# A hybrid attention block on one core: tail loads in pieces of 512 columns, more loaded ahead, query tiles in one store, first activations first

## The chip, the cores and the metric

One core of one Trainium2 chip runs the whole kernel. The metric is the device time of one execution in microseconds (us), lower is better; three executions of the kernel before gave 3302.88, 3305.68 and 3307.67 us.

## The reference

One layer of a hybrid block on 2048 tokens of width 1024, in float32:

```
h    = rmsnorm(x, norm1_g) * (1 + sc1) + sh1          # sc1, sh1, g1, ...: six rows of silu(c) @ w_ada + b_ada
proj = h @ w_in                                       # 1024 -> 3280 columns: aq ak av bq bk bv iq ik iw
A: 4 heads, two softmax maps each, softmax(q1 k1) - lam * softmax(q2 k2), times av, ALiBi, causal in chunks of 64
B: score[t,s] = sum over 16 heads of iw[t,h] * relu(iq[t,h] . ik[s]);  keep the 256 best keys of each query
   8 heads attend to these keys (one shared bk, bv), ALiBi
x = x + g1 * (concat(A, B) @ w_out)
x = x + g2 * (relu(h2 @ w_ff1)^2 @ w_ff2);  out = rmsnorm(x, final_g)
```

The factors on the norm and lambda parameters change only the inputs' values.

## The kernel before, in words

Matrices are multiplied as three products of two-part operands (high times high, high times low, low times high), so most tiles exist as a pair "hi" and "lo". Four stages follow each other; the instruction streams of the five engines are written out in order, and a stage ends when all of them are through.

**Index projection** (`index_projection`). x comes in four groups of 512 tokens (`xt`, two buffers). For each group ACT sums the squares (`squares`), DVE and ACT make 1/rms (`variance`, `root`, `inverse`), x is scaled, PE transposes it (`turn`, 8 slices k of 128 columns, in two parts of four), and DVE and ACT apply scale and shift and split the result into `ht_hi` and `ht_lo` (DVE's `activations`, ACT's `first_parts`, slice by slice, even slices made by DVE, odd by ACT). The scale and shift come from w_ada: DVE forms weighted sums (`ada_sums`, four first chunks of 512 columns), PE sums over partitions (`columns`), and `norm_cols` (L475) finishes them. `split_w` splits a weight tile on ACT and DVE. Then `unit(n, i, g)` multiplies weight tile i by token group g, 24 matmuls of 512 columns. There are nine weight tiles (the 1024 columns of iq, then ik, bv's upper part and iw in the others) and so 36 units; the first three tiles run group by group while the next group is being made. Each result is evacuated as hi (ACT) and lo (DVE, L437) and stored to DRAM by SP as four transfers of 64 rows (L333). SP's queue is in order: a store waits for its lo part, and the load of group 3 of x (L329) stands behind the stores of units 0 to 2. The last transfer of SP is that of the gates (L336).

**Indexing** (`indexing`). PE computes the remaining 17 tiles of the projection (544 steps of three matmuls, L1098) and, between them, the index scores of blocks 2 to 15 (a block is 128 queries): scores on PE (L1082), relu on ACT (L1143), weighted sum on DVE into `rank` (L1237); for blocks 2 to 11 a search for the 256th value in 24 rounds follows (ACT L1150, DVE L1258). SP loads `iq` in units of two heads (two transfers of 128 KB); unit n waits until unit n-3 has been used. POOL issues everything else: weights, stores of the tiles (four transfers each, L1023; the four av tiles one each into `scr.av`), the finished score rows of blocks 12 to 15 (`keep`, L1035), and when the last tile is stored `load_values` (L966: av by groups of 512 tokens with three of its four row tiles in one transfer, the fourth tile's columns 512 to 2047 in one, bv in three) and `load_ahead` (L987: queries of the first two attention units and the first 512 columns of bk and of six of the eight ak tiles). PE turns av and bv (`vturn`, L1114 to L1130; bv with 32 matmuls of 64 columns), ACT copies them (L1159). The order of all this on PE, ACT, DVE and POOL is written out by a planner (`indexing_streams`, `indexing_plan`): it starts, among the next steps of all streams, the one that can begin first, begins rounded to `INDEX_SLACK`, ties by a key that `INDEX_PLACES`, `REST_FROM`, `REST_PACE`, `ROUNDS` and `INDEX_MASK` set. The waits in the code keep it right whatever the plan.

**Attention** (`attention`). A second planner orders 16 blocks of 6 groups: scores (L3024), maxima (L3255), exponentials (L3091), the difference of the two maps (`combine`, L3265 to L3271), transposes (L3040), products with values (L3055, L3061), stores of the result to `dram_mix` (L2994). Score units of four heads are loaded by SP (L2933, two transfers of 256 KB, three buffers); SP also loads the missing keys (L2942). Unit 0 and unit 1 are those of group A, unit 2 the first of group B. The searches of blocks 12 to 15 run between: POOL fetches the row of block 12 as `rank_in` at once (L2975), DVE starts on it at L3167.

**Output and MLP** (`output_mlp`) is not touched.

## Time and profile before

| | us |
|---|---|
| median of three executions | 3305.68 |
| profiled execution, its own time | 3311.04 |
| span of its trace | 3309.3 |
| index projection, PE's first matmul to the next stage's | 10.0 to 296.4 |
| indexing, to the first matmul of attention | 296.4 to 961.9 |
| attention, output projection and MLP | 961.9 to 3309.3 |

A row of a timeline gives the start, the duration, the engine, the line, the operation, output and input, the count of merged instructions, and in brackets how long the engine was idle before and what released it. "SPq" and "POOLq" are queues that issue transfers; "PEq" is PE's own instruction queue. The granted clock of TensorE is either full (a 512-column matmul then shows 0.39 us and starts every 0.23 us) or half (0.63 us, every 0.43 us).

### The profile page before, as it was taken

The page shows a single profiled execution, that of the slowest core. Times are in us where ns is not written, and L with a number is a line of the kernel's source. Part 1 is how long each engine was busy: PE and PEld are TensorE (multiplying, and loading weights), DVE is VectorE, ACT ScalarE, POOL GpSimd, SP SyncE. Part 2 cuts the span into 40 slices and gives each one's busy share as a digit, 9 for nine tenths or more (in the row PEclk, how much of TensorE's full clock was granted, in tenths as well). Part 3 has the DMA queues.
Part 4 walks back from the last instruction along what each step waited for, and adds up shares of the span by engine and source line. Part 5 has one row for each costly group of instructions (what it writes and reads, how often), then busy time and mean ns, then how long its engine had stood idle before and what let it go on. Part 6 is the DMA issues. An engine that isn't in the chain of part 4 may idle for free. (4 is left out here: it accounts for less than half of the span.)

```text
span 3309.3 us, 44362 instructions
## 1 busy us (share of the span) xinstructions
PE 3132.8 (95%) x15808; PEld 2544.1 (77%) x15808; DVE 2439.7 (74%) x4302; ACT 1847.5 (56%) x3103; POOL 442.0 (13%) x713
## 2 busy tenths in 40 slices
PE   5899999999978999999999999999999999999998
PEld 4787888888756777777777787788778878888787
DVE  5544898999956687878776678787877875655676
ACT  4312888899768989898986334322432232222232
POOL 0011233012221000000000000221121210000321
PEclk9999999999979999999999999999999999999999
DMA  7476544233376432211111463544444456655555
GB/s 241 128 247 164 150 135 116 84 102 100 120 204 148 102 74 51 60 43 52 33 38 73 140 221 128 188 150 159 145 163 151 161 196 227 240 188 187 194 203 198
DMA packets 327002, 471.73 MB, mean 143 GB/s; under 512 B 25344, under 2 KB 214992, under 8 KB 326400
## 3 DMA queue, kind: packets, MB, share of 16 engines
q1 hardware_dynamic: 274768, 296.96, 30.0%
q0 software_dynamic: 52016, 171.96, 15.5%
q8 instruction: 125, 2.05, 0.3%
q14 instruction: 93, 0.76, 0.1%
HBM read 311.84 MB, written 156.98 MB: 142 GB/s over the span
## 5 line engine op out<-in xcount | busy, mean ns | idle before, releaser
L2513 PE MATMUL m_ps<-m_h,w_hi 128*128 128x512 f32 x1792 | 557.8, 393 | 20.0 <-DVE w_lo L2115 11.9
L2513 PEld LDWEIGHTS m_ps<-m_h,w_hi 128*128 128x128 f32 x1792 | 338.0, 189 | 95.8 <-DVE w_lo L2115 16.4
L1237 DVE SCALAR_TENSOR_TENSOR rank<-spare,iw,rank 128x1024 f32<-128x1024 f32 (+5 forms) x330 | 331.4, 1021 | 37.9 <-ACT spare L1143 31.3
L2526 PE MATMUL m_ps<-w_hi,a_hi 128*128 128x512 f32 x896 | 350.1, 391 | 6.3 <-DVE w_lo L2344 3.4
L2513 PE MATMUL m_ps<-m_h,w_lo 128*128 128x512 f32 x896 | 350.9, 392 | 0.0
L2526 PE MATMUL m_ps<-w_lo,a_hi 128*128 128x512 f32 x896 | 349.8, 390 | 0.0
L2526 PE MATMUL m_ps<-w_hi,a_lo 128*128 128x512 f32 x896 | 349.6, 390 | 0.0
L1143 ACT ACTIVATE spare<-isps 128x1024 f32<-128x1024 f32 (+5 forms) x352 | 277.6, 820 | 60.7 <-PE isps L1082 37.4
L1082 PE MATMUL isps<-ki,iq 128*128 128x512 f32 (+3 forms) x1216 | 291.4, 373 | 11.9 <-DMA iq<-dram_proj 8.8
L1082 PEld LDWEIGHTS isps<-ki,iq 128*128 128x128 f32 x1216 | 224.6, 190 | 67.4 <-DMA iq<-dram_proj 11.4
L1819 ACT ACTIVATE a_hi<-a_lo 128x2048 fp32r<-128x2048 f32 x56 | 107.3, 1917 | 279.3 <-DMA a_lo<-dram_aop 279.3
L3103 ACT ACTIVATE pt<-tps 128x512 f32<-128x512 f32 (+1 forms) x432 | 232.3, 584 | 55.3 <-PE ops L3055 26.6
L3040 PE MATMUL tps<-ident,probs 128*128 128x128 f32 x1632 | 236.6, 280 | 22.7 <-DVE probs L3271 17.6
L1781 ACT ACTIVATE w_hi<-w_raw 128x512 fp32r<-128x512 f32 x160 | 99.8, 625 | 264.1 <-DVE w_raw L2103 205.2
L3091 ACT ACTIVATE probs<-probs,stat 128x128 f32<-128x128 f32 (+15 forms) x192 | 233.1, 1217 | 20.0 <-DVE stat L3255 17.2
L3040 PEld LDWEIGHTS tps<-ident,probs 128*128 128x128 f32 x1632 | 182.1, 142 | 78.4 <-issue 35.2
L1150 ACT ACTIVATE below<-rank,tk 128x512 int8<-128x512 f32 (+9 forms) x210 | 230.4, 1100 | 19.2 <-DVE tk L1259 18.1
L2341 DVE TENSOR_TENSOR a_lo<-a_lo,a_hi 128x2048 fp32r<-128x2048 f32 x56 | 141.3, 2524 | 113.9 <-ACT a_hi L1819 113.8
L1098 PE MATMUL r_ps<-ht_hi,r_w_hi 128*128 128x512 f32 x544 | 216.4, 398 | 6.0 <-PEq L270 4.9
L1694 POOL DMA_DIRECT2D dram_aop<-a_out x224 | 121.0, 541 | 748.5 <-ACT a_out L1803 275.5
L1098 PE MATMUL r_ps<-ht_hi,r_w_lo 128*128 128x512 f32 x544 | 214.5, 394 | 0.0
L1098 PE MATMUL r_ps<-ht_lo,r_w_hi 128*128 128x512 f32 x544 | 213.8, 393 | 0.0
(317 smaller groups left out, 6594.4 us busy)
## 6 DMA issues: line engine op xcount, KB each, us to landing
w_raw<-in_w_ff SPq DMA_DIRECT2D x136, 512.0 KB, 5.5
dram_aop<-a_out POOLq DMA_DIRECT2D x224, 256.0 KB, 2.6
a_lo<-dram_aop SPq DMA_DIRECT2D x56, 1024.0 KB, 5.6
early_queries<-dram_proj SPq DMA_DIRECT2D x124, 256.0 KB, 4.3
iq<-dram_proj SPq DMA_DIRECT2D x224, 128.0 KB, 2.9
ada_w<-in_w_ada POOLq DMA_DIRECT2D x16, 1024.0 KB, 6.4
dram_proj<-r_ev_hi POOLq DMA_DIRECT2D x104, 128.0 KB, 2.6
dram_proj<-r_ev_lo POOLq DMA_DIRECT2D x104, 128.0 KB, 2.7
```

What stands on the lines that cost most here:

```text
L1082: mm = nc.tensor.matmul(sps[:, job.n % 2, a:b], iq[:, job.unit % IQU, job.head % 2, part, :], ki[:, job.c * SCH + a:job.c * SCH + b], star ...
L1098: mm = nc.tensor.matmul(ps[:, job.n % 4, :], a[:, i % 2, job.part, :], b[:, job.g, job.part, :], start=job.part == 0 and m == 0, stop=job. ...
L1143: nc.scalar.activation(spare[:, job.n % 2, 0:job.width], sps[:, job.n % 2, 0:job.width], ACT.Relu).then_inc(s_relu, 1)
L1150: nc.scalar.activation(below[:, q, 0:length].bitcast(I8), ranks[job.k % 3][:, 0:length], ACT.Sign, bias=tk[:, q, TK_NT:TK_NT + 1], accum_o ...
L1237: nc.vector.scalar_tensor_tensor(out=dst, in0=got, scalar=w, in1=dst, op0=ALU.mult, op1=ALU.add).then_inc(s_acc, 1)
L1694: pool.dma_start(scr.aop[op, row:row + P, half * GT:(half + 1) * GT], act_in[:, op, :]).then_inc(q_a[op], 16)
L2341: nc.vector.tensor_tensor(s_lo[:, c % RING], s_lo[:, c % RING].bitcast(F32), s_hi[:, c % RING].bitcast(F32), ALU.subtract).then_inc(c_sl, 1)
L2513: mm = nc.tensor.matmul(ps[:, b], w[:, w1_slot(n, j), k, :], hop[:, j, h, :, k, :], start=fresh and k == 0 and i == 0, stop=k == KH - 1 an ...
L2526: mm = nc.tensor.matmul(ps[:, t], a[:, c % RING, k, t * P:(t + 1) * P], w[:, c % RING, k, :], start=first and i == 0, stop=last and i == 2 ...
L3040: tr = nc.tensor.transpose(tps[:, job.turn % TR, (2 * kk + hh) * P:(2 * kk + hh + 1) * P], probs[:, g.heads[hh] % 4, (job.first + kk) * P: ...
L3091: nc.scalar.activation(row, row, ACT.Exp, bias=stat[:, job.hm % 8, 2:3], scale=-1.0, accum_out=stat[:, job.hm % 8, 3:4]).then_inc(s_exp, 1)
L3103: nc.scalar.activation(pt[:, job.slot % PT, 0:width], tps[:, job.of.turn % TR, 0:width], ACT.Copy).then_inc(s_te, 1)
```

## The change

Query tiles of the projection are kept in DRAM by part (`by_part`: 128 rows of hi, then 128 of lo) and stored by one transfer of 512 KB in place of four of 128 KB; the six tiles with keys, bv and iw keep four. The loads of queries read the new arrangement, with as many transfers and bytes as before. In the projection's start ACT takes the first activations before the squares of group 1, `inverse(0)` and `columns(3)` come earlier, and `split_w(0)` on DVE comes behind the first activation. The tail loads of indexing fetch the fourth av tile and bv in pieces of 512 columns; bv lies with hi on partitions 0 to 63 and lo on 64 to 127, and is turned by 16 matmuls with two identities stacked in place of 32. `load_ahead` takes three units, seven ak tiles and the score row of block 12. The planner's constants of indexing are new. `fac` is made by one scalar_tensor_tensor. Left out below: `stored_by`, the changed indices of `queries` and `iq` in loads and matmuls, and places in SBUF.

```diff
-INDEX_SLACK = 0.0347
-REST_FROM, REST_PACE, ROUNDS, INDEX_MASK = 75.86, 12.486, -34.794, 169.04
-INDEX_PLACES = dict(index=-17.19, relu=-566.8, add=26.95, chain0=-84.64, chain1=-82.32, keep=-267.36, split=258.6,
-                    lo=110.56, mm=-14.26, evac=-14.83, evac_lo=-191.95, store=-481.49, kept_mask=-573.36,
-                    weights=-212.32, vload=20.2, ahead=-14.8, vturn=-70.63, vcopy=31.74)
+INDEX_SLACK = 0.0636
+REST_FROM, REST_PACE, ROUNDS, INDEX_MASK = 132.07, 8.185, -26.461, 168.05
+INDEX_PLACES = dict(index=-10.95, relu=-518.06, add=-25.25, chain0=-91.79, chain1=-87.39, keep=-319.67, split=239.2,
+                    lo=191.27, mm=29.75, evac=-79.21, evac_lo=-185.88, store=-387.22, kept_mask=-566.03,
+                    weights=-221.42, vload=-82.91, ahead=56.8, vturn=-270.56, vcopy=-9.75)
...
+        self.by_part = self.proj.rearrange("(c m) r p t -> c (m r p) t", m=2)
...
+KEY_TILES = [*range(R_AK // P, R_AK // P + 4), R_BK // P, CT - 1]
+
+
+def stores_of(tile):
+
+    return 4 if tile in KEY_TILES else 1
+
+
+def store_tile(eng, scr, tile, tok, hi, lo, both, s):
+
+    if tile not in KEY_TILES:
+        eng.dma_start(scr.by_part[tile, :, tok].rearrange("(r p) t -> p r t", p=P), both.bitcast(F32)).then_inc(s, 16)
+        return
+    for part, src in enumerate((hi, lo)):
+        for half in range(2):
+            eng.dma_start(scr.proj[tile * P // DH + half, part, :, tok],
+                          src[half * DH:(half + 1) * DH, :].bitcast(F32)).then_inc(s, 16)
+
...
+        self.rank = sb("rank", [P, SEQ])
...
-        ev_hi = sb("ev_hi", [P, EV, GT], F32R)
-        ev_lo = sb("ev_lo", [P, EV, GT], F32R)
+        ev = sb("ev", [P, EV, 2, GT], F32R)
+        ev_hi, ev_lo = ev[:, :, 0, :], ev[:, :, 1, :]
...
-                    for part, src in enumerate((ev_hi, ev_lo)):
-                        for half in range(2):
-                            sp.dma_start(scr.proj[INDEX_TILES[i] * P // DH + half, part, :, g * GT:(g + 1) * GT],
-                                         src[half * DH:(half + 1) * DH, n % EV, :].bitcast(F32)).then_inc(s_st[n % EV], 16)
+                    store_tile(sp, scr, INDEX_TILES[i], slice(g * GT, (g + 1) * GT), ev_hi[:, n % EV, :],
+                               ev_lo[:, n % EV, :], ev[:, n % EV], s_st[n % EV])
...
-                squares(1, range(0, 2))
                 act.wait_ge(s_cols, 1)
-                first_parts(0, range(KT))
-                squares(1, range(2, TG))
+                first_parts(0, range(KT - 2))
+                squares(1, range(0, 1))
+                first_parts(0, range(KT - 2, KT))
+                squares(1, range(1, TG))
                 root(1)
...
-                def ada_sums(at, h):
+                def ada_sums(at, h, between=None):
...
+                        if between and k == (h + 1) * KH - 2:
+                            between()
...
+                        if g == 0 and k == 1:
+                            split_w(0)
...
-                ada_sums(2, 1)
-                inverse(0)
+                ada_sums(2, 1, lambda: inverse(0))
                 for h in range(2):
                     ada_sums(3, h)
-                split_w(0)
...
-                def turn(g, part):
+                def turn(g, part, halves=(0, 1)):
                     pe.wait_ge(s_xn, TG * (g + 1))
-                    for k in range(part * KT // 2, (part + 1) * KT // 2):
+                    first = part * KT // 2
+                    for k in range(first + halves[0] * KT // 4, first + (halves[-1] + 1) * KT // 4):
...
-                turn(0, 0)
+                turn(0, 0, (0,))
                 columns(3)
+                turn(0, 0, (1,))
                 turn(0, 1)
...
-EARLY_KEYS, EARLY_UNITS = 6, 2
+EARLY_KEYS, EARLY_UNITS = 7, 3
...
-    for n, (count, late) in enumerate(((2, 6.0), (2, 11.0), (1, 14.0), (1, 17.0), (3, 21.0))):
+    for n, (count, late) in enumerate(((2, 6.0), (2, 9.0), (2, 13.0), (2, 17.0), (4, 21.0))):
...
-    put("ahead", Step("ahead", "Q", 13.0, 9.0, REST_FROM + REST_PACE * (len(REST_TILES) + 6), [(loads[-1], -21.0)]))
+    put("ahead", Step("ahead", "Q", 16.0, 8.0, REST_FROM + REST_PACE * (len(REST_TILES) + 6), [(loads[-1], -20.0)]))
...
-        turn = put("vturn", Step("vturn", "PE", 0.55 if n < NB else 1.26, 0.163, where, after, n=n))
+        turn = put("vturn", Step("vturn", "PE", 0.55 if n < NB else 0.63, 0.163, where, after, n=n))
...
-        low_b = early.queries[0:DH, QU - 1].rearrange("p m r q -> p (m r q)")
+        def sparse_rows(g):
+
+            return early.ka[:, NG, g * GT:(g + 1) * GT] if g else early.ka[:, EARLY_KEYS - 1, GT:2 * GT]
+
...
-                    elif n == 1:
-                        pool.dma_start(early.kb[:, GT:].bitcast(F32), scr.av[3 * P:, GT:]).then_inc(s_vin[1], 16)
-                    elif n == NG:
-                        row = scr.proj[R_BV // DH]
-                        pool.dma_start(low_b.rearrange("p (r t) -> p r t", r=2).bitcast(F32),
-                                       row[:, :, 0:GT].rearrange("r p t -> p r t")).then_inc(s_vin[NG], 16)
-                        for part in range(2):
-                            pool.dma_start(early.ka[0:DH, NG + part, GT:].bitcast(F32),
-                                           row[part, :, GT:]).then_inc(s_vin[NG], 16)
+                    elif n < NG:
+                        tok = slice(n * GT, (n + 1) * GT)
+                        pool.dma_start(early.kb[:, tok].bitcast(F32), scr.av[3 * P:, tok]).then_inc(s_vin[n], 16)
+                    else:
+                        for g in range(NG):
+                            tok = slice(g * GT, (g + 1) * GT)
+                            pool.dma_start(sparse_rows(g).bitcast(F32),
+                                           scr.proj[R_BV // DH, :, :, tok].rearrange("r p t -> (r p) t")
+                                           ).then_inc(s_vin[NG], 16)
...
-                        row = early_units[n] // DH
-                        view = scr.proj[row:row + 4, :, :, 0:P].rearrange("m r p q -> p (m r) q")
+                        row = early_units[n] // P
+                        view = scr.by_part[row:row + 2, :, 0:P].rearrange("c (x p) q -> p (c x) q", p=DH)
                         for half in range(2):
-                            pool.dma_start(early.queries[half * DH:(half + 1) * DH, n].rearrange("p m r q -> p (m r) q")
+                            pool.dma_start(early.queries[half * DH:(half + 1) * DH, n].rearrange("p c r m q -> p (c r m) q")
                                            .bitcast(F32), view).then_inc(s_ahead, 16)
...
+                    pool.wait_ge(s_kept[(SPLIT - 2) % 3], 16)
+                    for a in range(0, P * (SPLIT + 1), GT):
+                        b = min(a + GT, P * (SPLIT + 1))
+                        pool.dma_start(early.rank[:, a:b], scr.ranks[0, :, a:b]).then_inc(s_ahead, 16)
...
-                                pe.wait_ge(s_idr, 1)
-                                pe.wait_ge(s_vin[NG], 48)
+                                pe.wait_ge(s_idr, 2)
+                                pe.wait_ge(s_vin[NG], 16 * NG)
                             for m in range(8):
                                 kt = 8 * (n - NB) + m
-                                for part in range(2):
-                                    if kt < 4:
-                                        rows = low_b[:, part * GT + kt * P:part * GT + (kt + 1) * P]
-                                    else:
-                                        rows = early.ka[0:DH, NG + part, kt * P:(kt + 1) * P]
-                                    mm = nc.tensor.matmul(ps[:, n % 4, m * DH:(m + 1) * DH], rows, ident_r[:],
-                                                          start=part == 0, stop=part == 1, skip_group_check=True)
+                                rows = sparse_rows(kt // 4)[:, kt % 4 * P:(kt % 4 + 1) * P]
+                                mm = nc.tensor.matmul(ps[:, n % 4, m * DH:(m + 1) * DH], rows, ident_r[:],
+                                                      start=True, stop=True, skip_group_check=True)
...
-                nc.scalar.activation(ident_r[:], keep.ident[0:DH, 0:DH], ACT.Copy).then_inc(s_idr, 1)
+                for half in range(2):
+                    rows = slice(half * DH, (half + 1) * DH)
+                    nc.scalar.activation(ident_r[rows, :], keep.ident[rows, rows], ACT.Copy).then_inc(s_idr, 1)
...
-                if job.kind == "fetch":
-                    if job.block > SPLIT:
-                        pool.wait_ge(s_mask, job.block - SPLIT)
+                if job.kind == "fetch" and job.block > SPLIT:
+                    pool.wait_ge(s_mask, job.block - SPLIT)
...
-                    dve.wait_ge(s_rank, 16 * (job.block - SPLIT + 1))
+                    if job.block > SPLIT:
+                        dve.wait_ge(s_rank, 16 * (job.block - SPLIT))
...
-                    then(nc.vector.tensor_scalar(fac[:], stat[:, a, 3:4], rinv[:, r, 1:2], keep.neg_lam[:],
-                                                 ALU.mult, ALU.mult))
+                    then(nc.vector.scalar_tensor_tensor(out=fac[:], in0=stat[:, a, 3:4], scalar=rinv[:, r, 1:2],
+                                                        in1=keep.neg_lam[:], op0=ALU.mult, op1=ALU.mult))
```

## Rows read from the trace of the kernel before

**Rows 1.** The page, engines: busy time, share of the span, instructions.
```profile
PE 3132.8 (95%) x15808; PEld 2544.1 (77%) x15808; DVE 2439.7 (74%) x4302; ACT 1847.5 (56%) x3103; POOL 442.0 (13%) x713
```

**Rows 2.** Windows: stretch, length, busy time by engine, clock, DMA share, GB/s.
```profile
150.00:200.00 50.00, 50.00 (x228) 40.70 (x227) 22.90 (x32) 7.53 (x11) 6.41 (x8) 1.00 0.75 243
...
296.40:961.00 664.60, 650.48 (x2972) 534.21 (x2972) 583.91 (x1161) 555.58 (x875) 159.25 (x278) 0.99 0.45 127
...
950.00:960.00 10.00, 9.85 (x71) 8.59 (x70) 7.15 (x6) 8.44 (x13) 0.56 (x1) 1.00 0.13 52
```

**Rows 3.** Timeline, start of the projection.
```profile
39.80 3.68 PE L605 MATMUL tps<-ident,xt_first 128*128 128x128 f32 x16 [2.52 <-ACT xt_first L397]
...
41.32 1.22 DVE L431 TENSOR_TENSOR w_lo<-w_raw,w_hi 128x1024 fp32r<-128x1024 f32 x1
...
43.27 1.71 PE L614 MATMUL col_psum<-ones,ada_sums 128*128 128x1 f32 x8
...
45.75 0.81 DVE L532 TENSOR_SCALAR u<-tps,cols 128x512 f32<-128x512 f32 x1 [0.29 <-DVE cols L473]
...
48.87 1.06 ACT L367 ACTIVATE ada_first<-xt 128x1024 f32<-128x1024 f32 x1 [6.95 <-DMA xt<-in_x]
...
51.10 0.61 ACT L386 ACTIVATE ht_hi<-u 128x512 fp32r<-128x512 f32 x1
...
55.71 0.78 PE L593 MATMUL ps<-ht_hi,w_hi 128*128 128x512 f32 x1
...
59.23 0.39 PE L593 MATMUL ps<-ht_hi,w_lo 128*128 128x512 f32 x1
...
61.17 0.69 DVE L536 TENSOR_TENSOR ht_lo<-u,ht_hi 128x512 fp32r<-128x512 f32 x1 [0.80 <-ACT ht_hi L386]
```

**Rows 4.** Timeline, the load of the last group of x and PE's wait.
```profile
92.32 0.59 SPq L329 DMA_DIRECT2D xt<-in_x  x1
...
101.21 1.06 ACT L367 ACTIVATE ada_first<-xt 128x1024 f32<-128x1024 f32 x1 [5.87 <-DMA xt<-in_x]
...
115.69 3.67 PE L605 MATMUL tps<-ident,xt 128*128 128x128 f32 x16 [3.96 <-DVE xt L516]
```

**Rows 5.** Timeline, from the projection to indexing.
```profile
294.02 1.23 SPq L333 DMA_DIRECT2D dram_proj<-ev_lo  x2
...
296.40 0.76 PE L1098 MATMUL r_ps<-ht_hi,r_w_hi 128*128 128x512 f32 x1 [4.90 <-PEq L270]
```

**Rows 6.** Timeline, PE in the tail of indexing.
```profile
931.87 2.85 PE L1082 MATMUL isps<-ki,iq 128*128 128x512 f32 x8 [3.24 <-DMA iq<-dram_proj]
...
943.00 1.90 PE L1082 MATMUL isps<-ki,iq 128*128 128x512 f32 x4 [4.72 <-DMA iq<-dram_proj]
...
957.52 2.84 PE L1130 MATMUL r_ps<-ident_v,early_ka 64*128 64x64 f32 x24
```

**Rows 7.** DMA queues, 925 to 930, then 930 to 935: packets, MB, share.
```profile
q0 software_dynamic: 392, 1.48, 91.6%
q1 hardware_dynamic: 392, 0.19, 14.5%
...
q0 software_dynamic: 205, 0.92, 91.2%
q1 hardware_dynamic: 204, 0.10, 14.0%
```

**Rows 8.** Timeline, start of attention.
```profile
963.18 0.54 POOL L2975 DMA_DIRECT2D rank_in<-dram_ranks  x1 [0.36 <-issue]
...
973.98 0.69 PE L3024 MATMUL sps<-early_kb,early_queries 128*128 128x128 f32 x2 [6.17 <-DMA early_queries<-dram_proj]
...
984.19 0.63 ACT L3115 ACTIVATE mixst<-ops,rinv 128x128 f32<-128x128 f32 x2 [3.15 <-DMA dram_mix<-mixst]
...
984.96 1.08 PE L3055 MATMUL ops<-pt,early_vb 128*64 128x256 f32 x2 [2.39 <-ACT mixst L3115]
```

**Rows 9.** Groups of instructions: busy us, mean ns, idle before.
```profile
L3268 DVE TENSOR_SCALAR fac<-stat,rinv,neg_lam 128x1 f32<-128x1 f32 x64 | 17.5, 273 | 2.3
```

50 lines of the change are left out of this document (25 added, 25 removed).

## The prediction

> **What bounds the kernel now.** I read the page first: PE is busy for 95% of the span [rows 1], so time is won where PE waits, where it runs at the lower of its two clocks, or where it is given less to do. Then I read the windows for such places: 50.00 us of 50 in the projection's even part, 650.48 of 664.60 us through indexing, at a mean granted clock of 0.99 [rows 2]. DVE has 583.91 and ACT 555.58 us in the same stretch, so neither is far below. Indexing is thus bound by PE except in its tail. Then timelines of the seams. Four of them have PE idle and are touched by the change: the projection's start [rows 3], its last group of x [rows 4], the step to indexing [rows 5], and the tail of indexing with the start of attention [rows 6 to 8]. MLP, a third of the span, is untouched, and nothing there depends on when it starts.
>
> **Start of the projection.** The first real matmul starts at 55.71 [rows 3]. Behind it stands ACT: the first slice of activations `u` is there at 45.75 + 0.81 = 46.56, but ACT splits it at 51.10 only, because in its order the squares of group 1 come first and these wait 6.95 us for x, which lands at 48.87. The change takes this wait away. What is late next: `u` itself. It waits for `columns(3)`, which PE does behind 16 transposes (39.80 to 43.27), while the sums it needs are ready at 41.32. With 8 transposes ahead of it and `inverse(0)` earlier, `columns(3)` begins at about 41.4 in place of 43.27; DVE then does not put `split_w(0)` (1.22) ahead, but that was hidden beside `columns(3)` anyway. So `u` starts at 45.75 - 1.85 = 43.9, and ACT splits at 44.7, 6.4 us earlier than 51.10. `split_w(0)` now stands behind the first `u`: 44.7 to 45.95, and holds the first low part back by 0.5 us (the high part is done at 44.7 + 0.61). The slices thus come 5.9 us earlier, the first matmul at about 49.8. Of slices 6 and 7 one group of squares is now ahead, 1.05 to 1.25 us: the last low part moves from 61.17 to 61.17 - 5.9 + 1.1 = 56.4. The clock: PE was at the lower level until 59.23, 3.5 us after the first matmul; the same 3.5 us at half speed from 49.8 give 53.3, 5.9 earlier, and the remaining matmuls (16 at 0.23, 3.7 us) then end at 57.0, just where the last low part (57.1) allows it, so unit 0 ends some 5.2 us earlier. x of group 1 is scaled at about 63 in place of 66.8, while PE wants it at 63.3: hidden, and 0.4 us late at worst. Term: -5.2; bounds: -3.5 (slices 6 and 7 and the scaling both late) and -6.4.
>
> **Last group of x.** SP issues this load at 92.32, behind the four transfers of unit 2's store; it lands after 8.9 us, ACT waits 5.87 us for it, and at the end of that chain PE waits 3.96 us at 115.69 [rows 4]. Three of four issues of that store go. One costs 1.23 / 2 = 0.6 us [rows 5], so the load starts 1.8 to 2.2 us earlier, and PE's wait falls to about 1.8. PE then did 16 transposes in 3.67 us at the lower clock, as in [rows 3], where full clock would make it about half. Whether 1.8 us of idling is short enough to keep the full clock no row tells; if it is, another 1.8 to 2.1 us go. Term: -2.2, the nearest row being the wait itself; bounds -1.5 and -4.3. The Trainium skill, "TensorE: Matmul & The Clock Gate", Part 1, says that idling is what sends the clock back and that this depends on when the gap comes; by it the shorter gap would more often keep full clock, and the sum would be -4. The 3.96 us gap with 3.67 us behind it agrees with the first half.
>
> **Step to indexing.** PE waits 4.90 us until 296.40, when SP has issued its last transfers [rows 5]. Three issues of 0.6 us fall away: -1.8, bounds -1.2 and -2.3. The store's own landing is later awaited with the gates' in one wait and moves with it. Between the first and the last unit the fewer issues are worth nothing: PE is full (50.00 of 50) [rows 2] and covers them.
>
> **The body of indexing.** The same 32 stores of query tiles become one transfer each; POOL is busy for 159.25 us of 664.60 and nobody on the path waits for it. The planner's new constants reorder the streams. By the keys the scores still go ahead of the projection's matmuls, and the search ahead of the sums, so most of the order stays. PE's work is the same and only its 14.1 us of idling [rows 2] could go, of which 8 belong to the tail. I take 0; bounds -5 (most of the rest goes) and +6 (1% of the stage, less than DVE's reserve of 66 us under PE makes impossible).
>
> **Tail of indexing.** PE waits 3.24 and 4.72 us for `iq` while POOL's mass of loads runs [rows 6]. The packets show how: from 925 to 930 the two queues moved 392 packets each, from 930 to 935 205 and 204 [rows 7]. They take turns packet by packet, so `iq`, cut in packets of 0.5 KB, gets as many turns as POOL's queue has packets, and these were 3.8 and 4.5 KB long. A unit of `iq` has 512 packets, 6.5 us at the first rate and 12.5 us at the second. In pieces of 512 columns the fourth av tile comes in packets of 2 KB in place of 6, bv in 512 packets in place of 192: about 580 more turns before the heavy queries, more than one unit. That says both waits shrink, the second least, since a third unit of queries (128 packets of 4 KB) now stands ahead too. I take 3 of the 8 us (bounds: 8 gone, 3 more). The last bv matmuls, 24 in 2.84 us [rows 6], halve with the others: 32 x 0.118 / 2 = 1.9 us less, with the copies of ACT waiting for them. Against this stands a new hold: the extra loads are 512 + 256 + 832 KB = 1.6 MB, at 334 or 204 GB/s [rows 7] 4.8 to 7.8 us. The transfers were through by 950 (share 0.13 after it) [rows 2]; now they last to 955 to 958, and POOL waits for them at the stage's end. PE's end would be 960.4 - 4.9 = 955.5. So of 4.9 us I count 4. Bounds: +2 (`iq` later by 3, bv's 1.9 kept, loads late) and -7. The Trainium skill, "DMA: Bandwidth & Descriptors", Bandwidth, speaks against cutting loads up: it wants 1 MiB a transfer and gives some 2 us fixed for each, by which three transfers of 256 KB for one of 768 KB would add about 4 us, and the tail's gain would be nothing. Here the engines are full to 91% on POOL's queue alone [rows 7], so fixed times lie beside other transfers.
>
> **Start of attention.** PE waits 6.17 us for the queries of the third unit, behind 832 KB of `rank_in` and keys [rows 8]. Both are now there beforehand: the wait goes. What is late next are the queries of the fourth unit: PE wants them about 7 us after the third, at 974 to 975 on the old clock, and SP issues them some 2 us into the stage; even 9 us to landing would do. ACT then waited 3.15 us for a store to land in the crowded queues, and PE 2.39 us for ACT [rows 8]; with 1.6 MB fewer in these 20 us half of that should go. Term: -6.2 - 1.3 = -7.5; bounds: -3 and -9.
>
> **The rest.** `fac`: 64 instructions of 273 ns, 17.5 us in all [rows 9], beside PE for the most part; 0, bounds -2 and +2. Two ACT copies for the stacked identities, 0.3 us at a time when ACT waits for weights: 0. The search's first instruction waits no longer, and did not wait before.
>
> **The sum.** -5.2 - 2.2 - 1.8 + 0 - 4 - 7.5 + 0 = -20.7 us. The profiled execution had 3311.04 us of its own; it becomes 3290.3. The median of the runs shown is 5.4 us below the profiled one, which gives 3285.
>
> **Rivals.** (1) The loads ahead hold the stage's end: the engines are through, POOL still waits for the last piece of the score row. For it: 1.6 MB more into queues at 91% [rows 7]. Against: 10 us with hardly a transfer before the end [rows 2]. The tail then gives +2 in place of -4: 3291. (2) Attention's start gives nothing: the wait moves to the fourth unit. For it: its queries share the queues with three keys. Against: 832 KB less ahead of it. 3285 + 7.5 = 3292. (3) All goes better: full clock kept at group 3 (-2), both `iq` waits gone and PE's idling in indexing too (-7): 3276. (4) Slower: the new order of indexing makes PE wait for DVE or ACT. Its place is 296 to 961, where PE now has a ready matmul nearly always [rows 2]; a loss of 3.1% of that stage, 20.7 us, is the point from which it decides, and with DVE at 88% and ACT at 84% of it, twice this is possible: 41 us, giving 3305.7 - 20.7 + 41 = 3326. For it: several constants changed by tens of blocks. Against: keys decide only among steps that begin within 0.06 us. (5) The first term fails, because PE's later waits in the projection (3.96 us) hang on DMA landing at a fixed time and not on PE: 3290.
>
> **How the numbers follow.** The forecast 0.52, its own range 3279 to 3291; rival 1 0.14, rival 2 0.11, rival 3 0.11, rival 4 0.06, rival 5 0.06. A measurement tells 0.2%, 6.6 us, from no change: faster is below 3299.1. The forecast, 1, 2, 3 and 5 are faster, but half of 1 and 2 could meet a loss of 5 us in the body of indexing, and some of those end within 0.2%: faster 0.86, same 0.08, slower 0.06. The range 3275 to 3297 leaves out rival 4, the upper end of 1 and 2 and the lower end of 3.
>
> **What would show it.** `ht_hi` first split near 44.7 and the first long matmul near 50; a wait of about 2 us or less before the transposes of the last group; 3 us between PE's last projection matmul and indexing, not 4.9; waits for `iq` in the tail under 5 us in all, 16 bv matmuls; no wait for queries of the third unit, and transfers ending within 3 us of the stage's end. It is wrong if the body of indexing has more PE idling than 6 us outside the tail, if a wait of over 4 us for other queries opens in attention, or if the four seams together give less than 12 us.

## The result and the profile after

The changed kernel takes 3286.02 us (median of 4 runs, 3284.53 to 3286.66), the kernel before beside it 3306.68 (4 runs, 3302.88 to 3308.01): the ratio is 0.9935, 95% interval [0.9924, 0.9947], 20.7 us less. Forecast were 3285 and the same 20.7 us. (Timed a second time, `e1_after` below, the difference of the medians was 22.6.) The execution that was profiled took 3285.41 us, span 3283.6, 25.7 less than the span before. Those 5 us more than the medians give are mostly the old trace's: traced a second time (`e3_before_again`, below), the kernel before had a span of 3305.6, and 22.0 us are left.

The page's engine line and windows of the changed kernel, against [rows 1, 2]. The second window runs from indexing's first matmul to attention's:

```profile
PE 3126.7 (95%) x15792; PEld 2535.0 (77%) x15792; DVE 2433.2 (74%) x4302; ACT 1847.0 (56%) x3104; POOL 401.4 (12%) x626
```

```profile
150.00:200.00 50.00, 50.00 (x229) 40.72 (x228) 26.86 (x36) 8.52 (x12) 7.19 (x9) 1.00 0.70 234
283.41:945.61 662.20, 647.57 (x2956) 529.05 (x2956) 582.49 (x1163) 556.24 (x879) 120.32 (x192) 0.99 0.43 130
940.00:945.00 5.00, 0.76 (x7) 0.64 (x6) 0.00 (x0) 1.29 (x3) 0.00 (x0) 0.68 1.00 393
```

PE has the same work less 16 matmuls and is as full as before in both long stretches. POOL is busy 38.9 us less in indexing, where the stores now take fewer issues; PE is no fuller for it. The third row is new: 5 us before attention in which PE does almost nothing and the transfers run at 393 GB/s. Not all of these are loads ahead. The DMA view of the same 5 us has 461 packets, 1.97 MB, and only 349 of them lie under 8 KB:

```profile
DMA packets 461, 1.97 MB, mean 393 GB/s; under 512 B 93, under 2 KB 93, under 8 KB 349
```

The other 112 have the 8 KB of a row of the last score row's store (block 15, 128 rows of 2048 columns, `keep`), which POOL issued at 937.51. They are 0.92 MB, nearly half of the bytes; the stage's end doesn't wait for this store, but it shares the engines with the loads that it does wait for.

The timeline of the changed kernel from the projection's start to its end, against [rows 3 to 5]:

```profile
40.72 1.87 PE L641 MATMUL col_psum<-ones,ada_sums 128*128 128x1 f32 x8 [1.13 <-DVE ada_sums L492]
...
43.10 0.81 DVE L560 TENSOR_SCALAR u<-tps,cols 128x512 f32<-128x512 f32 x1
...
44.01 0.63 ACT L409 ACTIVATE ht_hi<-u 128x512 fp32r<-128x512 f32 x1 [2.75 <-DVE u L560]
...
48.55 0.48 PE L619 MATMUL ps<-ht_hi,w_hi 128*128 128x512 f32 x1
48.87 0.39 PE L619 MATMUL ps<-ht_lo,w_hi 128*128 128x512 f32 x1
...
54.92 0.69 DVE L564 TENSOR_TENSOR ht_lo<-u,ht_hi 128x512 fp32r<-128x512 f32 x1 [0.64 <-ACT ht_hi L409]
...
92.67 1.06 ACT L390 ACTIVATE ada_first<-xt 128x1024 f32<-128x1024 f32 x1 [3.83 <-DMA xt<-in_x]
...
107.14 1.97 PE L632 MATMUL tps<-ident,xt 128*128 128x128 f32 x16 [1.39 <-DVE xt L542]
...
282.03 0.36 SPq L113 DMA_DIRECT2D dram_proj<-ev  x1
...
283.41 0.77 PE L1130 MATMUL r_ps<-ht_hi,r_w_hi 128*128 128x512 f32 x1 [2.77 <-PEq L295]
```

`ht_hi` is split 7.1 us earlier than in [rows 3], the first long matmul comes 7.2 us earlier. PE's wait for the last group of x is 1.39 us in place of 3.96 [rows 4], and the 16 transposes behind it take 1.97 us in place of 3.67. The step to indexing costs 2.77 us in place of 4.90 [rows 5], with one transfer of `ev` on SP where there were four. Indexing starts 13.0 us earlier.

The timeline at the tail and at attention's start, against [rows 6, 8], and then the group of `fac`, against [rows 9]:

```profile
921.95 3.78 PE L1114 MATMUL isps<-ki,iq 128*128 128x512 f32 x8 [2.76 <-DMA iq<-dram_proj]
...
938.78 1.97 PE L1158 MATMUL r_ps<-ident_v,early_ka 128*128 128x64 f32 x16
...
945.04 0.29 DVE L3174 TENSOR_TENSOR early_table<-early_table,early_diagonal 128x128 f32<-128x128 f32 x1 [7.83 <-PEq L965]
...
945.61 2.97 PE L3054 MATMUL sps<-early_ka,early_queries 128*128 128x128 f32 x10 [4.86 <-ACT stack L3113]
```

```profile
L3299 DVE SCALAR_TENSOR_TENSOR fac<-stat,rinv,neg_lam 128x1 f32<-128x1 f32 x64 | 14.1, 220 | 2.3
```

The last turn of bv ends at 938.78 + 1.97 = 940.75, where it was 960.36. Then PE stands for 4.86 us, and DVE for 7.83: no engine starts attention before the loads ahead have landed. No wait for a third unit's queries is left. `fac` takes 220 ns in place of 273.

### The profile page after: what moved, and what is told of

Its sections match the earlier page's. It is cut to its first block and busy times, and to the rows that moved or that the text cites. A ratio compares the mean times of both kernels' runs of the same rounds, so it can differ in the third digit from the quotient of the medians.

```text
span 3283.6 us, 44143 instructions
## 1 busy us (share of the span) xinstructions
PE 3126.7 (95%) x15792; PEld 2535.0 (77%) x15792; DVE 2433.2 (74%) x4302; ACT 1847.0 (56%) x3104; POOL 401.4 (12%) x626
## 3 DMA queue, kind: packets, MB, share of 16 engines
q8 instruction: 125, 2.05, 0.3%
```

## The experiments

Each kernel was timed in 5 rounds. Beside the first four the kernel before had 3308.68 us (9 runs), beside the next four 3307.78 (11), beside the last four 3307.95 (15). A table first, in which every trace is cut in three: when indexing starts; PE's time in it (first matmul to the last turn of bv); the rest to the end of the span. For the kernel before that end is 957.52 + 2.84 [rows 6].

| kernel | indexing starts | PE in indexing | rest | median | ratio, interval |
|---|---|---|---|---|---|
| before | 296.40 | 664.0 | 2348.9 | 3306.68 | |
| e3_before_again | 296.07 | 665.3 | 2344.3 | 3308.14 | 1.0004 [0.9995, 1.0013] |
| changed | 283.41 | 657.3 | 2342.8 | 3286.02 | 0.9935 [0.9924, 0.9947] |
| e1_after | 283.02 | 659.1 | 2343.2 | 3286.13 | 0.9930 [0.9916, 0.9944] |
| e1_undo_start | 289.64 | 658.3 | 2341.8 | 3294.53 | 0.9957 [0.9943, 0.9971] |
| e1_four_stores | 289.72 | 656.9 | 2344.5 | 3290.57 | 0.9944 [0.9930, 0.9957] |
| e1_rank_wait_late | 284.16 | 656.6 | 2340.1 | 3283.28 | 0.9928 [0.9915, 0.9942] |
| e2_old_plan | 283.33 | 666.1 | 2336.8 | 3290.24 | 0.9949 [0.9934, 0.9964] |
| e2_no_ahead | 284.33 | 655.7 | 2344.1 | 3287.94 | 0.9942 [0.9925, 0.9959] |
| e2_rank_fetched_late | 286.20 | 658.3 | 2343.5 | 3287.88 | 0.9937 [0.9922, 0.9952] |
| e2_one_piece | 287.13 | 660.1 | 2340.9 | 3287.08 | 0.9936 [0.9920, 0.9952] |
| e3_later_waits | 284.01 | 659.4 | 2343.1 | 3289.84 | 0.9946 [0.9932, 0.9959] |
| e3_old_fac | 285.16 | 656.8 | 2340.1 | 3285.68 | 0.9937 [0.9923, 0.9950] |
| e3_before_new_plan | 294.88 | 671.0 | 2354.2 | 3321.89 | 1.0038 [1.0024, 1.0052] |

The intervals reach about 3 to 6 us to each side, so a part worth 2 us doesn't show in a ratio. Where a median is said to rise or fall below, it is against the 3286.13 of `e1_after`.

**The changed kernel again.**

> The changed kernel itself, timed beside the others and the kernel before. If the 25.7 us between the two traces are the whole effect, the medians differ by 25; if the kernel before was only unlucky in its profiled execution, by 20 to 21.

It came out at 3286.13 us, 22.6 below the kernel before beside it: nearer to the second reading than to the first. The seams up to indexing lie within 0.7 us of the changed kernel's, bv ends 1.4 us later, and attention's first scores waited 6.30 us in place of 4.86. So the hold of one and the same code varies by 1.4 us.

**The projection's start undone.**

```diff
-                act.wait_ge(s_cols, 1)
-                first_parts(0, range(KT - 2))
-                squares(1, range(0, 1))
-                first_parts(0, range(KT - 2, KT))
-                squares(1, range(1, TG))
+                squares(1, range(0, 2))
+                act.wait_ge(s_cols, 1)
+                first_parts(0, range(KT))
+                squares(1, range(2, TG))
```

with `inverse(0)`, `split_w(0)` and `columns(3)` back at their old places.

> Changed kernel, with only the order at the projection's start as it was (squares of group 1 first, split_w(0), inverse(0) and columns(3) in their old places). My account, by the sum of waits: first long matmul back near 55.5 and 6.5 us slower than the changed kernel. Rival, that later parts of the projection hang on transfers landing at fixed times: the first matmul moves, but the time by 3 us or less.

```profile
55.22 0.78 PE L618 MATMUL ps<-ht_hi,w_hi 128*128 128x512 f32 x1
...
88.11 3.38 PE L631 MATMUL tps<-ident,xt_first 128*128 128x128 f32 x16 [3.96 <-DVE xt_first L541]
...
289.64 0.76 PE L1128 MATMUL r_ps<-ht_hi,r_w_hi 128*128 128x512 f32 x1 [2.77 <-PEq L295]
```

The first long matmul is back at 55.22, group 2 is turned 6.4 us later than in `e1_after` (81.74), and indexing starts 6.6 us later. The median rose by 8.4, and the rival is out. The order of the start is worth 6.4 to 6.6 us at its own place and the kernel keeps it to the end.

**Four stores for a query tile in the projection.** The destination stays, cut in four:

```diff
-                    store_tile(sp, scr, INDEX_TILES[i], slice(g * GT, (g + 1) * GT), ev_hi[:, n % EV, :],
-                               ev_lo[:, n % EV, :], ev[:, n % EV], s_st[n % EV])
+                    store_in_four(sp, scr, INDEX_TILES[i], slice(g * GT, (g + 1) * GT), ev_hi[:, n % EV, :],
+                                  ev_lo[:, n % EV, :], s_st[n % EV])
```

> Changed kernel, with each tile of the index projection stored by SP in four transfers again, to the same places. My account: the load of the last group of x starts 1.8 to 2.2 us later, PE waits over 3 us before its transposes and is then at the lower clock (another 1.7 to 2.3 us), and the step to indexing is 2 us longer: 6 us slower in all. Rival, that the kept clock was chance and not the shorter wait: 4 us slower, and the 16 transposes still take 1.9 to 2.0 us.

```profile
109.39 3.68 PE L643 MATMUL tps<-ident,xt 128*128 128x128 f32 x16 [3.96 <-DVE xt L553]
...
289.72 0.76 PE L1141 MATMUL r_ps<-ht_hi,r_w_hi 128*128 128x512 f32 x1 [4.89 <-PEq L306]
```

Both waits of before are back to the hundredth, 3.96 and 4.89, and with the first of them the half clock on the transposes. Indexing starts 6.7 us later than in `e1_after`: 2.6 at the last group, 2.1 at the step, and the 1.9 between them is the clock. The median rose by 4.4. One trace can't tell the rival from my account, that the kept clock was chance: the table of nine traces below does that.

**The wait for the score row moved to its use.**

```diff
-                        pool.dma_start(early.rank[:, a:b], scr.ranks[0, :, a:b]).then_inc(s_ahead, 16)
+                        pool.dma_start(early.rank[:, a:b], scr.ranks[0, :, a:b]).then_inc(early.s_rank, 16)
```

> Changed kernel, but the score row loaded ahead has a semaphore of its own on which DVE waits where its search begins, and the stage's end no longer waits for it. My account (rival 1 of the prediction in part: PE now idles 4.86 us at the stage's end because the loads ahead have not landed): 832 KB at some 390 GB/s, the last in the queue, so the stage ends 2.1 us sooner and the kernel is 2 us faster. Rival, that the end is set by something else (the store of the last row, the keys): no change.

```profile
943.67 2.97 PE L3054 MATMUL sps<-early_ka,early_queries 128*128 128x128 f32 x10 [2.94 <-ACT stack L3113]
```

PE's wait fell from 4.86 and 6.30 to 2.94, and the median by 2.9 us: the size that was expected, but the interval doesn't tell it from nothing.

**The planner's old constants in the changed kernel.**

```diff
-INDEX_SLACK = 0.0636
+INDEX_SLACK = 0.0347
```

and the other constants of the change, likewise.

> Changed kernel with the planner's old constants for indexing (the costs of the streams stay new). My account: the body of indexing is bound by PE either way, 0 within 2 us. Rival: the new constants are what brings the tail forward (waits for iq 4.3 us in place of 8.8): 3 to 6 us slower, with iq waits of 7 us or more.

The waits of PE from the projection's end on, engine, line, waited for, then us in total, times, longest; the first fence is `e2_old_plan`, the second the changed kernel:

```profile
PE isps L1114 <- DMA iq<-dram_proj: 7.1, 6, 4.4
...
PE sps L3054 <- ACT stack L3113: 2.4, 1, 2.4
```

```profile
PE sps L3054 <- ACT stack L3113: 4.9, 1, 4.9
PE isps L1114 <- DMA iq<-dram_proj: 4.3, 2, 2.8
```

The rival held: waits for `iq` of 7.1 us, the median 4.1 us above `e1_after`'s, PE's time in indexing back at 666.1 us, the value of before. But the rest is the shortest of all, 2336.8. A part of that is the clock. These are windows of the 60 us behind the last turn of bv, `e2_old_plan`, then `e3_before_again`; the granted clock is the third number from the end:

```profile
949.46:1009.46 60.00, 47.13 (x237) 35.81 (x238) 36.11 (x171) 46.60 (x150) 7.58 (x15) 0.77 0.78 186
```

```profile
961.33:1021.33 60.00, 44.35 (x197) 33.92 (x197) 30.85 (x152) 40.47 (x131) 6.58 (x13) 0.64 0.79 180
```

With full clock as 1 and half as 0.5, a mean of 0.77 is 28 of the 60 us at half clock, 0.64 is 43. The changed kernel has 0.66 there (41 us), `e2_no_ahead` 0.72 (34).

**No more loaded ahead than before** (two units, six keys, the row of scores fetched in attention).

```diff
-EARLY_KEYS, EARLY_UNITS = 7, 3
+EARLY_KEYS, EARLY_UNITS = 6, 2
```

> Changed kernel with two units, six ak tiles and no score row loaded ahead, as before; the pieces of 512 columns stay. My account: PE's 4.86 us of idling at the stage's end falls to about 1.6, attention's start loses the 6.2 us for the third unit and the 2.4 to 3 us behind the store: 5 to 6 us slower in all. Rival, that the gain of attention's start came from elsewhere (fac, the order of stores): the third unit's wait is back, yet under 3 us slower.

```profile
941.60 0.66 PE L3051 MATMUL sps<-early_ka,early_queries 128*128 128x128 f32 x4 [1.55 <-ACT stack L3110]
...
954.19 0.69 PE L3051 MATMUL sps<-early_kb,early_queries 128*128 128x128 f32 x2 [6.79 <-DMA early_queries<-dram_proj]
```

The hold is gone (1.55 us) and the wait for the third unit's queries is back (6.79, against 6.17 in [rows 8]). The median rose by 1.8 us, inside the interval, where 5 to 6 were expected: the rival's number, though not for its reason. Loading ahead took 6.79 us of waiting away and put 3.3 us of hold in its place, 4.7 in the repetition. The clock was higher here (0.72 against 0.66, as said), so this trace's rest is the shorter for it.

**The score row alone fetched in attention.**

```diff
-                        pool.dma_start(early.rank[:, a:b], scr.ranks[0, :, a:b]).then_inc(s_ahead, 16)
```

> Changed kernel with only the score row of block 12 fetched at attention's start, as before. My account: the stage ends 2.1 us sooner, and the 832 KB then stand beside the queries of the fourth and fifth unit, where nothing waits for 6 us: within 1.5 us of the changed kernel. Rival, that it was the row and not the place in the order that held up the third unit's queries before: 3 us or more slower, with a new wait of PE for queries or of ACT for a store.

```profile
959.34 1.89 DVE L3194 TENSOR_REDUCE tk<-early_rank 128x1 f32<-128x1664 f32 x1 [3.06 <-DMA early_rank<-dram_ranks]
```

PE's wait at attention's start was 4.06 us, against 4.86 and 6.30. The search then waited 3.06 us for the row, and PE stood 5.56 us for DVE behind it, where the changed kernel has 2.53. The time is the same within 2 us.

**The fourth av tile in one piece again.**

```diff
-                        pool.dma_start(early.kb[:, tok].bitcast(F32), scr.av[3 * P:, tok]).then_inc(s_vin[n], 16)
+                        pool.dma_start(early.kb[:, GT:].bitcast(F32), scr.av[3 * P:, GT:]).then_inc(s_vin[1], 16)
```

> Changed kernel with columns 512 to 2047 of the fourth av tile loaded in one transfer again (rows of 6 KB). My account, that the two queues take turns packet by packet: 256 packets of POOL's queue fewer, so iq gets 256 turns fewer and PE waits for it 2 to 3 us more; of that 0 to 2 us reach the time, since the stage's end waits for the loads anyway. Rival, that pieces are worth nothing: iq waits as in the changed kernel, 4.3 us.

Two waits for `iq` of 2.79 and 2.43 us, 7.3 us in all over the stage against 4.3 in the changed kernel and 3.0 to 4.4 in the eight other traces that have both the new plan and the pieces. PE's time in indexing was 1 to 3 us longer than in the changed kernel and its repetition, the median 1 us. The waits grew as expected, but the count behind them was wrong. The pages count POOL's packets over the whole program, the changed kernel, then this one:

```profile
q0 software_dynamic: 51024, 172.74, 15.1%
```

```profile
q0 software_dynamic: 50928, 172.74, 15.1%
```

That is 96 packets fewer for the same bytes, and not 256: rows of 2 KB don't travel one to a packet (1.57 MB in 440 packets, 3.6 KB each, in the changed kernel from 915 to 920). At 440 packets in 5 us, 96 turns are an estimated 1.1 us of the 3 to 4; where the rest comes from isn't shown. The Trainium skill, "DMA: Bandwidth & Descriptors", Bandwidth, has the rule to make transfers large. No cost of the pieces shows here: in one piece the median is 1 us higher, inside the interval.

**Each load awaited where it is used.** Three semaphores in place of one; the stage's end waits for unit 0 and four keys only. The order of the loads changes with it: unit 0 and four keys, unit 1 and three keys, unit 2 and bk, the row, where the changed kernel loads all three units first.

```diff
-                pool.wait_ge(s_ahead, 16 * (1 + EARLY_KEYS + 2 * EARLY_UNITS + (P * (SPLIT + 1) + GT - 1) // GT))
+                pool.wait_ge(s_ahead, 16 * (2 + 4))
...
+                        if unit in (1, 2):
+                            pe.wait_ge(early.s_later[unit - 1], 16 * (2 + EARLY_KEYS - 4 if unit == 1 else 3))
```

> The changed kernel, with the end of indexing held only by what attention's first unit needs (its queries and four key tiles); the rest of the loads ahead (unit 1's queries and three keys, unit 2's queries and bk, the score row) is awaited where it is first used, each on a semaphore of its own. If the hold at the stage's end is what swallowed the gain of the tail, PE's wait ahead of attention's first scores falls from 4.9 us (6.3 in its repetition) to the 1.6 that it had with few loads ahead, the third unit finds its queries there, and the time is 3 to 4.5 us below the changed kernel, about 3282. Rival: the bytes are what is short, not the place of the wait; PE then meets the same wait at its second or third unit and 0 to 1 us is left.

```profile
944.92 2.81 PE L3064 MATMUL sps<-early_ka,early_queries 128*128 128x128 f32 x10 [1.55 <-ACT stack L3123]
...
953.33 0.69 PE L3064 MATMUL sps<-early_ka,early_queries 128*128 128x128 f32 x2 [4.47 <-DMA early_ka<-dram_proj]
```

The hold went (1.55) and stood again 8 us later, 4.47 us, for a key, and at 966.20 PE waited 3.02 us more behind ACT. The median, 3289.84, is 3.7 above `e1_after`'s. The rival held: with this order of loads the bytes are short, not the place of the wait. In its windows, 940 to 965 in steps of 5 us, the DMA engines are full throughout, at shares of 1.02 to 1.17 (the column before the last); two of them:

```profile
940.00:945.00 5.00, 3.44 (x30) 3.12 (x29) 0.40 (x2) 4.52 (x11) 0.56 (x1) 1.00 1.03 206
...
950.00:955.00 5.00, 1.68 (x8) 1.68 (x9) 0.84 (x6) 0.72 (x4) 0.00 (x0) 0.50 1.03 365
```

**The new constants alone, in the kernel before.** The reverse of `e2_old_plan`'s edit, and nothing else.

> The kernel before with the planner's new constants alone. By the run with the old constants in the changed kernel, they are worth 4 us: PE's time from the first matmul of indexing to the last should fall from 664.0 us towards 657, and as no new loads hold the stage's end here, the time falls by 4 to 7 us against the kernel before, to about 3302. Rival, as I had it in the prediction: the constants give nothing by themselves, only with the smaller pieces and the single stores; then 0 to 1 us.

Neither: 3321.89 us, 13.9 slower than the kernel before, its interval clear of 1. From its timeline, PE, POOL, PE:

```profile
931.96 0.40 PE L1098 MATMUL r_ps<-ht_hi,r_w_lo 128*128 128x512 f32 x1
...
940.04 0.79 POOL L972 DMA_DIRECT2D early_ka<-dram_av  x1 [2.68 <-DMA dram_proj<-r_ev_lo]
...
973.21 2.10 PE L3024 MATMUL sps<-early_ka,early_queries 128*128 128x128 f32 x7 [7.33 <-ACT stack L3083]
```

The plan puts the last product of the last tile at 931.96, where `e3_before_again` has it at 906.55; the tail loads start at 940.04 in place of 915.47, and attention waits 7.33 us for them. The planner's keys weigh against the costs that it books, and the change also books a store of a query tile at 0.55 in place of 2.15. That this is what moves the last tile is argued and not shown.

**The old instruction for `fac`.**

```diff
-                    then(nc.vector.scalar_tensor_tensor(out=fac[:], in0=stat[:, a, 3:4], scalar=rinv[:, r, 1:2],
-                                                        in1=keep.neg_lam[:], op0=ALU.mult, op1=ALU.mult))
+                    then(nc.vector.tensor_scalar(fac[:], stat[:, a, 3:4], rinv[:, r, 1:2], keep.neg_lam[:],
+                                                 ALU.mult, ALU.mult))
```

> The changed kernel with the old instruction for fac (two scalars by one tensor_scalar). From the start of attention to the end the changed kernel took 9.4 us less than the kernel before, and the wait for the third unit's queries explains 5.5 of them. My theory: fac's 64 instructions lie beside PE, and undoing them costs 0 to 1 us of time, though DVE's busy time rises by 64 x 0.05 = 3.2 us. Rival: they stand in a chain that PE waits for, and explain the rest: 3 us or more.

```profile
L3299 DVE TENSOR_SCALAR fac<-stat,rinv,neg_lam 128x1 f32<-128x1 f32 x64 | 17.5, 273 | 2.3
```

273 ns are back, 3.4 us of DVE, and the median is 3285.68: no difference that shows. Its trace had the shorter rest (2340.1).

**The kernel before, traced again.**

> The kernel before, profiled again. Its only trace was 3 to 4 us longer than its median. If this was attention's part, the time from the first scores to the end should be about 2344 here in place of 2347.4, and the seams ahead of it the same within 1 us (first long matmul 55.7, PE's wait 3.96 ahead of the last group's transposes and half clock behind it, indexing at 296.4). Rival: the seams vary from run to run, and then the comparison of the two traces by seams is worth less than the medians.

```profile
114.97 3.68 PE L605 MATMUL tps<-ident,xt 128*128 128x128 f32 x16 [3.96 <-DVE xt L516]
...
962.89 2.97 PE L3024 MATMUL sps<-early_ka,early_queries 128*128 128x128 f32 x10 [1.55 <-ACT stack L3083]
...
974.55 0.69 PE L3024 MATMUL sps<-early_kb,early_queries 128*128 128x128 f32 x2 [5.78 <-DMA early_queries<-dram_proj]
```

The seams are the old ones within 1 us (indexing starts at 296.07, behind the same 4.90), and the rest is 4.6 us shorter. So of the 6 us by which the first pair of traces differs there, 4.6 belong to one execution.

## Why the prediction was right

The sum was right to the tenth in the pair of runs, some 2 us short in the repetition (22.6), and that is more than its terms were. By traces, and against both traces of before, the projection gave 12.7 to 13.0 us where 9.2 were forecast, and all behind it 9.3 to 12.7 where it was 11.5.

**Start, -5.2.** Right in mechanism, -6.4 to -6.6 in size (`e1_undo_start`; 88.88 to 82.38 at group 2 in the pair). Two small steps failed, both for the better. `u` began at 43.10 and not 43.9. And I had the first 3.5 us of matmuls at half clock again: from 48.87 on they took 0.39 us [rows 3 have the first such at 59.23]. PE's longest gap between 42.45 and that matmul was 0.44 us, where before it had stood for 1.73 and 4.65 us between transposes; that this kept the clock up is argued, but `e1_undo_start`, with the gaps back, shows the 0.78 us again. With the clock up, PE waits 0.53, 0.55 and 0.37 us for the last low parts: the low part (54.92) is now what is late.

**Last group of x, -2.2.** The wait fell by 2.57 us, at the place 2.05 earlier beyond the first term, as worked out. The clock, which I left open, was kept: another 2.3 us until indexing. The length of the wait doesn't decide whether it is kept. Nine traces have the same projection (all of the changed kind but the two that undo a part of it); PE waited 1.39 to 3.48 us there, by when x landed, six kept full clock and three lost it:

| | waits of PE, us | transposes to indexing, us |
|---|---|---|
| kept (16 in 1.97) | 1.39, 1.52, 1.85, 1.86, 3.25, 3.48 | 176.2 to 176.3 |
| lost (16 in 3.60 to 3.68) | 2.20, 2.98, 3.15 | 177.9 to 179.1 |

3.48 us kept the clock and 2.20 lost it, and `e1_undo_start` kept it with 3.35. The Trainium skill, "TensorE: Matmul & The Clock Gate", Part 1, has the moment of the change depend on when the work falls, so that it differs from run to run; these traces agree. In `e1_four_stores`, the kernel before, its repetition and `e3_before_new_plan`, 3.96 us lost it each time. So this gain is there in six executions of nine, and the changed kernel's own trace was one of the six.

**Step to indexing, -1.8.** Measured -2.1 (4.90 to 2.77).

**Body of indexing and its tail, 0 and -4.** Here the split was wrong. PE's time in indexing fell by 5 to 8 us (664.0 and 665.3 to 657.3 and 659.1), of which 1.8 are the bv matmuls, as worked out, and 4.5 the waits for `iq` (8.8 to 4.3), where I had taken 3. This last was luck in part. I counted about 580 more turns for `iq`, from packets of 2 KB; `e2_one_piece` shows that cutting the fourth av tile adds 96 packets and not 256. And with the old constants the smaller pieces and the shorter bv brought nothing, 666.1. I had put the new order at 0 because PE is full in the body; the place where an order decides is when the last tile is stored and how many `iq` units are still to come while the loads run. The queues show it. The packets, 915 to 920 and then 925 to 930, changed kernel first, then `e2_old_plan`:

```profile
q0 software_dynamic: 440, 1.57, 90.2%
q1 hardware_dynamic: 440, 0.21, 15.6%
...
q0 software_dynamic: 347, 1.13, 102.2%
q1 hardware_dynamic: 103, 0.05, 4.1%
```

```profile
q0 software_dynamic: 446, 1.54, 89.3%
q1 hardware_dynamic: 439, 0.21, 15.6%
...
q0 software_dynamic: 292, 0.95, 90.5%
q1 hardware_dynamic: 292, 0.14, 17.8%
```

Both kernels share turn by turn, as in [rows 7]. In the new order the `iq` units are through before 930 and POOL's queue has the engines alone; in the old one they go on sharing past 940 (455 and 456 packets from 935 to 940). The Trainium skill, "DMA: Bandwidth & Descriptors", Queues, rings and completion order, has the engines go round the queues by packets. The equal counts agree, if the profile's packets are the page's: it has several descriptors in one, and no row tells.

**The hold.** This is the step that failed. I had transfers end at 955 to 958 with PE's end at 955.5, a hold of about 1 us more; PE was done at 940.75 and they lasted until about 945, so it was 3.3 us more than before (4.86 against 1.56), and 4.7 in the repetition. Rival 1's mechanism thus came, but not its sum of +2: from indexing's first matmul to attention's the kernel still takes 662.20 us in place of 665.53, -3.3 (-1.4 in the two repetitions, 665.39 and 666.82), where I had -4. I had also left out the store of the last score row. In the kernel before it ran alone, with the share of 0.13 of [rows 2]; now it falls among the loads with half of the bytes. What the hold would be without it wasn't tried.

**Start of attention, -7.5.** The wait of 6.17 us went, as said, and no wait for a fourth unit came: rival 2 is out. From attention's first matmul to the end of the span the changed kernel and its repetition take 2338.0 and 2336.9 us, the kernel before 2347.4 and 2342.7: -4.7 to -10.5. But from the end of bv on, hold included, the rest is 1.1 to 1.5 us shorter than in `e3_before_again`, 6.1 against the first trace. What the prediction didn't see is that the loads which save this wait are what the stage's end then waits for. Before, the DMA engines were idle ahead of that end, [rows 2] 950 to 960 at a share of 0.13, and full behind it. With PE's end 8 us nearer to the loads that stretch is gone even without the extra loads (`e2_no_ahead` has 1.01 from 935 to 940, ahead of PE's end at 940.05), and 1.6 MB more at 393 GB/s are 4.1 us, about what the hold grew by. With the old plan the stretch was still there: `e2_old_plan` has shares of 0.27 and 0.00 from 940 to 950, so its hold of 2.42 us isn't made by the loads.

Whether the gain of the new order and that of the loads ahead add up is another question, and the runs don't decide it. By traces, all against `e3_before_again`: the new plan without loads ahead has -9.6 in indexing and -0.2 behind it, the loads ahead with the old plan +0.8 and -7.5. That makes 16.5 for the two apart. Both together have -7.3 to -12.7 over the five traces that differ only ahead of indexing or in `fac` (changed, `e1_after`, `e1_undo_start`, `e1_four_stores`, `e3_old_fac`). But the -7.5 is one trace with 28 us at half clock behind bv in place of 43. Later in attention, from the 25th store of its result to MLP's first matmul, 24 us at half clock by the traces' clock records (`e1_four_stores`, `e2_one_piece`) took 957.8 and 957.9 us and 17 us (the changed kernel, `e2_old_plan`, `e3_later_waits`) 954.8 to 955.0. At that price the 15 us less are worth an estimated 7, an upper bound, since PE idles more at attention's start. By medians, with 13 us taken off for the projection, the new plan alone has some 7 us, the loads alone 5, both 8 to 10, each known to 4 to 6 us to either side. So that the two draw on one account is argued, from the hold and from `e3_later_waits`, and not shown by the sums.

**The rest, 0.** `fac` costs nothing that shows either way. Rival 4, a worse order, came true only where the new constants met the old kernel. Rival 5 is out: the later wait moved with PE.

That the sum held is thus partly luck: some 3.6 us more came from the front than forecast and, if the medians' 20.7 is the whole, as much less from behind. What stays open: whether the constants' misfit in the kernel before hangs on the booked cost of a store; how much of the 4 us by which attention's rest varies between executions is the clock; what the last score row's store costs at the stage's end; and the single stores of indexing and the shorter turn of bv, which weren't undone by themselves.

## What to carry to other kernels

Before loads are moved ahead of a stage's end, find the stretch in which the DMA engines idle there, as it will be after the change and not before it, and put every transfer into it, stores that nobody waits for too: 1.6 MB ahead took some 6 us of waiting out of attention and gave 3.3 to 4.7 back as a hold. Moving a wait to the place of use doesn't help while these engines are full: in `e3_later_waits` it came back 8 us later, and the one such move that lowered the median (`e1_rank_wait_late`) did so by 2.9 us, less than the runs can tell. Constants that were tuned for a planner belong to the kernel that they were tuned with: the same ones gave some 4 us in one and took 14 in the other. And in one trace a stage can lie 4 us off, partly by the clock: trace the kernel before twice when a few us are to be explained, and compare the granted clock of the stretches before a difference is put down to the edit.

## What the hardware showed beyond that

Nine traces of one and the same projection start indexing between 283.02 and 287.13 us. The 4.1 us are made by two things in a row: the transposes of the last group start at 106.75 to 108.18, by when x landed, and behind that wait PE's clock is lost or not (up to 2.8 us). That is over half of the spread of the medians of these kernels (3283 to 3290).

The granted clock in the windows can be missing where a trace starts. In the kernel before, 52 to 60 us shows 1.00, while the matmul in it took 0.78 us [rows 3]. `e1_undo_start`, with the same order and the same 0.78 us, has 0.50 from 52 to 56. Windows of PE, the kernel before and then `e1_undo_start`, the clock behind the busy time:

```profile
52.00:56.00 4.00, 3.18 (x13) 1.00 0.00 0
```

```profile
52.00:56.00 4.00, 3.63 (x14) 0.50 0.00 0
```

Durations of one form are the surer sign of the two.
